# The odd chunks of the rwkv chunk stage kept on exchanged partition halves

## The chip, the cores and the metric

One core of a Trainium2 chip runs the kernel. The metric is the time of one execution on the device in microseconds (us); for several runs the median is given.

## What is computed

Twelve layers over 256 tokens of width 1024, in fp32. Each layer is a mixer and a feed-forward part; two of the mixers (rwkv, r = 0 and 1) are the recurrence that the change touches. Cut to its core, per head of 64:

```python
def step(state, inp):
    r_t, w_t, k_t, v_t, kk_t, a_t = inp
    sa = einsum('bhvk,bhk->bhv', state, kk_t)
    state = state * w_t - sa * (kk_t * a_t) + v_t * k_t      # outer products
    return state, einsum('bhvk,bhk->bhv', state, r_t)
_, y = lax.scan(step, zeros(B, 16, 64, 64), (rh, wh, kh, vh, kk, a))
y = ((y - mu) * rsqrt(var + eps)) * ln_w + ln_b             # per head
y = y + sum(rh * kh * r_k) * vh
out = (y * g) @ w_out
```

## The kernel before, in words

The layers run one after the other; weights stream in 512 KB units over the SP queue into rings, ScalarE and VectorE split each into a high and a low part, and TensorE runs three matmuls of 128x128 by 256 for each pair of blocks. In an rwkv layer the scan over 256 tokens is replaced by four chunks (CHN) of CH = 64 tokens. Sixteen heads of 64 are laid out in pairs: a tile [128, 8, 64] holds heads 2n on partitions 0 to 63 and 2n+1 on 64 to 127, so every product of the chunk stage is sixteen products of 64x64 (each_head, slices h), one for each n and half. In fp32 each is two weight loads and two matmuls in the trace. A product that reads its operands from half a and writes half b of PSUM uses the quarter (a, b) of the array. Most groups use h for both: they alternate between quarters (0,0) and (1,1).

The stage, in the order in which rwkv_pe (L301) issues it, by hand, on TensorE:
- to_tokens (L427), 12 groups: v, k and b of four chunks turned by the identity into banks B[0] to B[3]; ScalarE's tokens (L857, copies at L863) brings them to v_tok, kb_tok, bb_tok. Groups 4 to 7 wait for kb_done (VectorE, L1170), 8 to 11 for bb_done.
- score_part (L453, matmuls at L467): per chunk four half groups of 64x128; VectorE's mask (L1180, at L1182) multiplies them into scb and sck, and adds the unit matrix (L1188) and the turned level 0 (L1191) after part 1. Chunks 0 and 1 come first, the eight parts of chunks 2 and 3 two to a level of chunks 0 and 1.
- levels: the inverse of a unit triangular 64x64 matrix is built by doubling. level_product (L494) gives L·X for chunks a and a+1, the even chunk on (h, h), the odd one on (h, other(h)), so that successive matmuls go round all four quarters; VectorE's factor (L1193) multiplies by the level's mask into Qc; level_update (L509) makes the new X; ScalarE's copy_x (L866, at L869) brings it to Xc for even, then for odd; level_turned (L527) turns it and copy_turned (L871, at L874) copies it to XTc. level_product and level_turned wait for both copy_x.
- the chain over the chunks: right (L549), solve (L566), outputs_known (L577), outputs (L589), state (L599), with VectorE's carry (L1199) after each state, and the head norm of each chunk's result (head_mean, centre, centred_square, head_square, deviation, gained, normed). It lies between the levels of chunks 2 and 3, in an order written out by hand at L669 to L719. The queues of ScalarE (L911 to L982) and VectorE (L1239 to L1299) are written out by hand too, and each engine works strictly in its order. gn_std, st_ready, u_ready and the like are semaphores that count through both layers.

All of the stage is straight code without loops: some 1900 matmuls and as many weight loads in a layer, each an instruction of its own. After it, out_unit (L627) starts when the last norm is done.

```python
                for n, h in each_head():
                    even = mm(b0[h, n, :], scb[a][h, n, CH:2 * CH], Xc[a][h, n, :], start=True, stop=True)
                    odd = mm(b1[other(h), n, :], scb[a + 1][h, n, CH:2 * CH], Xc[a + 1][h, n, :], start=True, stop=True)
```

Of the kernel before, what the change touches and what calls it, by code (L numbers as in the profile page):

```python
# [145 lines left out]
def build_program(nc, layers, x_in, wa, wd, tab_in, vec_in, na_in, out):  # L146
# [6 lines left out]
    with ctx:  # L153
# [55 lines left out]
        for n in ("const_loaded tab_loaded x_loaded x_added sq_ready ssum_ready std_ready h_ready a_used d_used "  # L209
# [8 lines left out]
                  "v_final rk_ready rk_sum bonus_ready gain_ready tok_mm tok_ready score_mm score_ready lt_ready xt_ready "  # L218
# [59 lines left out]
        def score_bank(c, i):  # L278
            return level_bank(c, i % 3) if c < 2 else B[6 + i % 2]
# [21 lines left out]
        def rwkv_pe(pe, L, product):  # L301
# [114 lines left out]
            def each_head():  # L416
                for n in range(KT):
                    for e in range(2):
                        yield n, slice(HD * e, HD * e + HD)
# [3 lines left out]

            def ident_of(h):
                return T("ident")[h, h]

            def to_tokens(i):  # L427

                c, j = i % CHN, i // CHN
                if i >= 4:  # L430
                    pe.wait_ge(s["tok_ready"], 12 * r + i - 3)
                b = eight(B[i % 4][:, :])
                for n, h in each_head():
                    src = (qkv[h, 16 + n, tok(c)], qkv[h, 8 + n, tok(c)], oT[h, n, tok(c)])[j]
                    last = mm(b[h, n, :], src, ident_of(h), start=True, stop=True)  # L435
                last.then_inc(s["tok_mm"], 1)
# [4 lines left out]
            for i in range(4):  # L441
                to_tokens(i)
            pe.wait_ge(s["kb_done"], r + 1)
            for i in range(4, 8):
                to_tokens(i)
            pe.wait_ge(s["bb_done"], r + 1)
            for i in range(8, 12):
# [5 lines left out]
            def score_part(c, i):  # L453

                g = 4 * (c - 2) + i
                if g in (0, 1):
                    pe.wait_ge(s["bonus_ready"], 4 * r + 3 + g)
                elif g > 1:
                    pe.wait_ge(s["score_ready"], 16 * r + 7 + g)
                elif i == 3:  # L460
                    pe.wait_ge(s["score_ready"], 16 * r + 4 * c + 1)
                b = score_bank(c, i)[:, :].rearrange("p (n t) -> p n t", n=4)
                for n in range(4):
                    for h in (slice(0, HD), slice(HD, P)):
                        m = 4 * (i % 2) + n
                        left = qkv[h, 8 + m, tok(c)] if i >= 2 else oT[h, m, tok(c)]
                        last = mm(b[h, n, :], left, qkv[h, m:m + 25:24, tok(c)], start=True, stop=True)  # L467
                last.then_inc(s["score_mm"], 1)
# [2190 lines left out]
```

## Time and profile before

| | us |
|---|---|
| median of 3 runs (lowest, highest) | 2318.24 (2310.27, 2321.24) |
| the profiled execution | 2314.36 |
| its span, first to last instruction | 2312.3 |
| TensorE busy in it | 2195.0 (95%) |
| VectorE, ScalarE busy | 1548.9, 1209.7 |
| mean granted clock of TensorE | 0.989 |

The span runs from the first to the last instruction of the profiled execution; 2.1 us of that execution lie around it. Times on the rows are counted from the start of the span. Matmuls overlap in their pipeline, so a busy TensorE isn't one at its peak, and "issue" as the end of an idle time means that the engine waited for nothing that the profile shows. x is a count of instructions; mean times are in ns. The chunk stages lie at 134.5 to 262 us and at 1291 to 1415 us.

### The profile page before, as it was taken

To read this page: it belongs to the slowest core of one execution; us is meant where nothing else is said; L and a number is where in the kernel's file an instruction comes from. 1 tells how busy PE (TensorE), PEld (TensorE's weight loads), DVE (VectorE), ACT (ScalarE), POOL (GpSimd) and SP (SyncE) were. 2 spreads that over 40 slices of the span, in tenths; PEclk is the share of its full clock that TensorE was granted. 3 is DMA by queue.
4 is the path that set the end of the run, shared out by engine and by line. 5 is a ranking of instruction groups with operands and counts; after the bars stand their busy time and mean duration, and the time that the engine had idled before them with its cause. 6 is when DMAs were issued, how large, how long until landed. Compare 5 with 4: busy or idle time off the path is not lost. (4 is left out here: it accounts for less than half of the span.)

```text
span 2312.3 us, 55947 instructions
## 1 busy us (share of the span) xinstructions
PE 2195.0 (95%) x23136; PEld 2101.8 (91%) x23136; DVE 1548.9 (67%) x2397; ACT 1209.7 (52%) x2065; POOL 36.3 (2%) x51
## 2 busy tenths in 40 slices
PE   6898899999999999999989988999999999999998
PEld 6887799999999988899978878999998999888998
DVE  7753565566655688665588635655776777876776
ACT  5734454455544447644468335544676444776443
POOL 0000000000000011000000000000100000100000
PEclk9899999999999999999989999999999999999999
DMA  5310354534455433355433103555334554434553
GB/s 204 128 48 4 111 190 164 191 128 130 168 180 188 144 119 128 124 202 188 159 101 128 48 5 111 191 180 187 133 111 137 188 194 155 146 119 143 185 190 109
DMA packets 88436, 327.16 MB, mean 141 GB/s; under 512 B 9808, under 2 KB 9936, under 8 KB 87632
## 3 DMA queue, kind: packets, MB, share of 16 engines
q1 hardware_dynamic: 87984, 322.66, 41.3%
q8 instruction: 129, 2.11, 0.4%
q0 software_dynamic: 288, 2.10, 0.3%
q14 instruction: 35, 0.29, 0.0%
HBM read 323.67 MB, written 1.05 MB: 140 GB/s over the span
## 5 line engine op out<-in xcount | busy, mean ns | idle before, releaser
L2122 PE MATMUL bank<-h_split,w_split 128*128 128x256 f32 x3176 | 913.1, 287 | 12.9 <-DVE h_split L2341 7.2
L2123 PE MATMUL bank<-h_split,w_split 128*128 128x256 f32 x3176 | 898.3, 283 | 0.0
L2124 PE MATMUL bank<-h_split,w_split 128*128 128x256 f32 x3176 | 897.8, 283 | 0.0
L2310 DVE TENSOR_TENSOR w_split<-ring_a,w_split 128x1024 fp32r<-128x1024 f32 x474 | 568.2, 1225 | 194.6 <-ACT w_split L2207 193.0
L2122 PEld LDWEIGHTS bank<-h_split,w_split 128*128 128x128 f32 x3176 | 603.3, 190 | 24.8 <-DVE h_split L2341 11.3
L2123 PEld LDWEIGHTS bank<-h_split,w_split 128*128 128x128 f32 x3176 | 599.1, 189 | 1.4
L2124 PEld LDWEIGHTS bank<-h_split,w_split 128*128 128x128 f32 x3176 | 598.3, 188 | 0.0
L2207 ACT ACTIVATE w_split<-ring_a 128x1024 fp32r<-128x1024 f32 x474 | 483.3, 1050 | 44.1 <-PE bank L636 23.7
L2144 PE MATMUL bank<-act_split,d_split 128*128 128x256 f32 x1008 | 285.3, 283 | 3.8 <-DVE act_last L2402 2.4
L2145 PE MATMUL bank<-act_split,d_split 128*128 128x256 f32 x1008 | 285.1, 283 | 0.0
L2146 PE MATMUL bank<-act_split,d_split 128*128 128x256 f32 x1008 | 285.0, 283 | 0.0
L2274 ACT ACTIVATE work<-work 128x256 f32<-128x256 f32 x88 | 36.9, 419 | 347.8 <-DVE work L2380 347.8
L2144 PEld LDWEIGHTS bank<-act_split,d_split 128*128 128x128 f32 x1008 | 193.1, 192 | 4.6 <-DVE act_last L2402 2.8
L2146 PEld LDWEIGHTS bank<-act_split,d_split 128*128 128x128 f32 x1008 | 193.1, 192 | 0.0
L2145 PEld LDWEIGHTS bank<-act_split,d_split 128*128 128x128 f32 x1008 | 192.9, 191 | 0.0
L2380 DVE TENSOR_TENSOR work<-bank,work 128x512 f32<-128x512 f32 x132 | 91.0, 689 | 151.3 <-PE bank L2124 150.7
L2377 DVE TENSOR_TENSOR d_split<-ring_d,d_split 128x1024 fp32r<-128x1024 f32 x126 | 153.6, 1219 | 2.5 <-ACT d_split L2271 2.5
L2271 ACT ACTIVATE d_split<-ring_d 128x1024 fp32r<-128x1024 f32 x126 | 131.5, 1044 | 0.0
L2277 ACT ACTIVATE work<-work 128x256 f32<-128x256 f32 x44 | 18.4, 418 | 179.6 <-DVE work L2394 179.6
L2398 DVE TENSOR_TENSOR work<-work 128x256 f32<-128x256 f32 x132 | 56.2, 426 | 64.0 <-ACT work L2274 42.7
L2402 DVE TENSOR_TENSOR act_split<-work,act_split 128x256 fp32r<-128x256 f32 x126 | 53.6, 426 | 61.0 <-ACT act_split L2280 61.0
L2280 ACT ACTIVATE act_split<-work 128x256 fp32r<-128x256 f32 x126 | 52.6, 418 | 62.0 <-DVE work L2398 62.0
(292 smaller groups left out, 3243.7 us busy)
## 6 DMA issues: line engine op xcount, KB each, us to landing
ring_a<-wa SPq DMA_DIRECT2D x474, 512.0 KB, 4.0
ring_d<-wd SPq DMA_DIRECT2D x132, 512.0 KB, 4.3
tab_sb<-tab SPq DMA_DIRECT2D x1, 2384.0 KB, 13.3
hT<-na POOLq DMA_DIRECT2D x2, 1024.0 KB, 5.1
xT<-x SPq DMA_DIRECT2D x1, 1024.0 KB, 4.9
out<-xT SPq DMA_DIRECT2D x1, 1024.0 KB, 3.9
vec_sb<-vec SPq DMA_DIRECT2D x1, 288.0 KB, 4.9
tab_sb<-tab SPq DMA_DIRECT2D x1, 65.0 KB, 4.7
```

The costliest lines, as they stand in the source:

```text
L2122: mm(dst, w[:, 0, ks], x[:, 0, k, :], start=(k == 0), stop=False)
L2123: mm(dst, w[:, 0, ks], x[:, 1, k, :], start=False, stop=False)
L2124: last = mm(dst, w[:, 1, ks], x[:, 0, k, :], start=False, stop=(k == KT - 1))
L2144: mm(o, w[:, 0, ms], x[:, 0, :], start=(first and m % 2 == 0), stop=False, skip_group_check=True)
L2145: mm(o, w[:, 0, ms], x[:, 1, :], start=False, stop=False, skip_group_check=True)
L2146: return mm(o, w[:, 1, ms], x[:, 0, :], start=False, stop=final, skip_group_check=True)
L2207: A(w_split[:, u % 4, 0, :], ring_a[:, u % 4, :], ACT.Copy).then_inc(s["w_hi"], 1)
L2271: A(d_split[:, q, 0, :], ring_d[:, q, :], ACT.Copy).then_inc(s["dn_hi"], 1)
L2310: v.tensor_tensor(w_split[:, u % 4, 1, :], ring_a[:, u % 4, :], w_split[:, u % 4, 0, :].bitcast(f32), ALU.subtract).then_inc(s["w_lo"], 1)
L2377: v.tensor_tensor(dd[:, 1, :], ring_d[:, q, :], dd[:, 0, :].bitcast(f32), ALU.subtract).then_inc(s["dn_lo"], 1)
L2380: v.tensor_tensor(work[:, 2 * q:2 * q + 2, :], B[4 + q][:, :].rearrange("p (a b) -> p a b", a=2), inv_rms().unsqueeze(1).broadcast_to([P, ...
L2398: v.tensor_tensor(work[:, 2 * q + 1, :], work[:, 2 * q, :], work[:, 2 * q + 1, :], ALU.mult)\
```

## The change

The odd chunks' tokens (v_tok, kb_tok, bb_tok) and scores (scb, sck) are kept on exchanged halves: head 2n on partitions 64 to 127 and 2n+1 on 0 to 63. to_tokens and score_part now make two chunks at once, an even one on (h, h) and an odd one on (h, other(h)), matmul by matmul in turn. What then reads odd tokens or scores takes them from side(c, h), and in odd chunks a sum in PSUM has parts from different quarters: such parts are separated by a wait of TensorE for its own earlier part (parts_done). In right, outputs_known and state of odd chunks the order of parts changes with it. VectorE copies the odd chunk's second and third token blocks (5, 7, 9, 11) and the odd chunks' new X (copy_x), which ScalarE did before. The scores of chunks 2 and 3 are made in one group after each of four level updates.

```diff
@@ score_bank
-            return level_bank(c, i % 3) if c < 2 else B[6 + i % 2]
+            return level_bank(c, i % 3) if c < 2 else B[6 + c % 2]
@@ to_tokens
                 if i >= 4:
-                    pe.wait_ge(s["tok_ready"], 12 * r + i - 3)
-                b = eight(B[i % 4][:, :])
+                    pe.wait_ge(s["tok_ready"], 8 * r + (i - 2 if i < 8 else i // 2 + 1))
+                if i >= 8:
+                    pe.wait_ge(s["tok_side"], 4 * r + (i - 6) // 2)
+                b0, b1 = eight(B[i % 4][:, :]), eight(B[i % 4 + 1][:, :])
                 for n, h in each_head():
...
+                    even = mm(b0[h, n, :], block(i % CHN), ident_of(h), start=True, stop=True)
+                    odd = mm(b1[other(h), n, :], block(i % CHN + 1), ident_of(h), start=True, stop=True)
@@ score_part
+                    even = mm(b0[h, n, :], left(a), qkv[h, m:m + 25:24, tok(a)], start=True, stop=True)
+                    odd = mm(b1[other(h), n, :], left(a + 1), qkv[h, m:m + 25:24, tok(a + 1)], start=True, stop=True)
@@ level_zero
-                    pe.wait_ge(s["score_ready"], 16 * r + 4 * c + 4)
+                    pe.wait_ge(s["score_ready"], 16 * r + 7 + c)
@@ right
+                    for n, h in each_head():
+                        g = side(c, h)
+                        last = mm(b[h, n, :], sck[c][g, n, CH:2 * CH], v_tok[g, c, n, :],
+                                  start=(n == 0), stop=(c == 0), skip_group_check=True)
+                    if c % 2:
+                        last.then_inc(s["parts_done"], 1)
+                if c and second:
+                    if c % 2:
+                        parted(c if c == 1 else 4)
@@ outputs_known
                 if c:
                     for n, h in each_head():
+                        last = mm(y_of(c, h, n), state_[h, n, :], qkv[h, n, tok(c)],
+                                  start=(n == 0 or (c == 3 and n == 4)), stop=False, skip_group_check=True)
+                    if c % 2:
+                        last.then_inc(s["parts_done"], 1)
+                        parted(2 if c == 1 else 5)
@@ state
+                    if c == 1:
+                        last.then_inc(s["parts_done"], 1)
+                        parted(3)
@@ order on TensorE
-            for c in (0, 1):
-                for i in range(4):
-                    score_part(c, i)
+            for i in range(4):
+                score_part(0, i)
...
                 level_update(0, lv)
-                score_part(2 + (lv - 1) // 2, (lv - 1) % 2 * 2)
+                score_part(2, lv - 1)
                 level_product(0, lv + 1)
                 level_turned(0, lv)
-                score_part(2 + (lv - 1) // 2, (lv - 1) % 2 * 2 + 1)
...
             level_product(2, 2)
+            right(1, second=False)
             level_turned(2, 1)
-            right(1)
+            right(1, first=False)
...
             state(2)
+            right(3, second=False)
             outputs(2)
-            right(3)
+            right(3, first=False)
@@ order on ScalarE
-            for i in range(12):
+            for i in (0, 1, 2, 3, 4, 6, 8, 10):
                 tokens(i)
...
                 copy_x(0, lv)
-                copy_x(1, lv)
@@ VectorE
+            def copy_x(c, lv):
+                q = 2 * r + c // 2
+                dve.wait_ge(s["xn_mm1"], 4 * q + lv)
+                v.tensor_scalar(Xc[c], eight(level_bank(c, 1)[:, :]), 1.0, None, ALU.mult)\
+                    .then_inc(s["xn_ready1"], 1)
@@ order on VectorE
-            for c in (0, 1):
-                for i in range(4):
-                    mask(c, i)
+            for i in (5, 7, 9, 11):
+                tokens(i)
+            for i in range(4):
+                mask(0, i)
+                mask(1, i)
...
             for lv in range(1, 5):
-                mask(2 + (lv - 1) // 2, (lv - 1) % 2 * 2)
+                copy_x(1, lv)
+                mask(2, lv - 1)
                 factor(0, lv + 1)
                 factor(1, lv + 1)
-                mask(2 + (lv - 1) // 2, (lv - 1) % 2 * 2 + 1)
+                mask(3, lv - 1)
...
             carry(0)
+            copy_x(3, 1)
             factor(2, 2)
             factor(3, 2)
             centre(0)
             gained(0)
+            copy_x(3, 2)
             factor(2, 3)
             factor(3, 3)
             normed(0)
             carry(1)
+            copy_x(3, 3)
             factor(2, 4)
             factor(3, 4)
             centre(1)
+            copy_x(3, 4)
             factor(2, 5)
```

## Rows read from the trace of the kernel before

**Rows 1.** Windows: stretch, us, busy us (instructions) by engine, clock, DMA share, GB/s.
```profile
core 0: us, PE busy (x) PEld busy (x) DVE busy (x) ACT busy (x) POOL busy (x), PEclk, DMA share, GB/s
147.00:162.00 15.00, 14.51 (x293) 11.92 (x288) 11.64 (x18) 1.42 (x2) 0.00 (x0) 1.00 0.01 3
190.00:240.00 50.00, 41.82 (x1604) 36.93 (x1600) 14.65 (x23) 19.40 (x35) 0.00 (x0) 1.00 0.02 4
```
**Rows 2.** Timeline of the tokens: start, us, engine, line, count, idle before and releaser.
```profile
134.46 7.54 PEld L435 LDWEIGHTS bank<-tab_sb,qkv 64*64 64x64 f32 x256
135.50 1.23 DVE L1170 TENSOR_TENSOR qkv<-qkv,ring_d 128x1024 f32<-128x1024 f32 x1
...
145.92 0.60 ACT L863 ACTIVATE hT<-bank 128x512 f32<-128x512 f32 x1 [0.34 <-PE bank L435]
...
146.57 1.96 PE L467 MATMUL bank<-qkv,oT 64*64 64x128 f32 x32 [0.70 <-ACT hT L863]
```
**Rows 3.** Windows within one level_product, for its line L504, then for L505.
```profile
164.50:165.50 1.00, 0.93 (x31) 0.96 (x32) 1.00 0.00 0
...
164.50:165.50 1.00, 0.92 (x31) 0.93 (x32) 1.00 0.00 0
```
**Rows 4.** DMA view of 190 to 240 us, then of 178 to 181 in 40 slices.
```profile
q8 instruction: 13, 0.21, 1.7%
...
GB/s 0 218 0 0 0 0 0 0 0 0 0 0 0 0 0 0 0 0 0 0 0 0 0 0 0 0 0 0 0 0 0 0 0 0 0 0 0 0 0 0
```
**Rows 5.** Timeline of TensorE: restarts after an idle time that ends in "issue".
```profile
180.64 0.21 PE L534 MATMUL bank<-tab_sb,planes 64*64 64x64 f32 x1 [1.76 <-issue]
...
186.22 0.27 PE L504 MATMUL bank<-planes 64*64 64x64 f32 x1 [0.67 <-issue]
...
189.57 0.65 PE L467 MATMUL bank<-qkv 64*64 64x128 f32 x8 [0.95 <-issue]
...
223.67 0.27 PE L505 MATMUL bank<-planes 64*64 64x64 f32 x1 [0.52 <-issue]
...
227.56 0.63 PE L593 MATMUL bank<-planes,work 64*64 64x64 f32 x15 [1.70 <-issue]
...
236.76 0.21 PE L534 MATMUL bank<-tab_sb,planes 64*64 64x64 f32 x1 [1.77 <-issue]
...
1378.31 0.85 PE L613 MATMUL bank<-work,hT 64*64 64x64 f32 x22 [0.34 <-issue]
...
1381.81 0.21 PE L535 MATMUL bank<-tab_sb,planes 64*64 64x64 f32 x1 [1.07 <-issue]
```
**Rows 6.** Timeline of VectorE: first and last masks of chunks 0 and 1.
```profile
147.71 0.69 DVE L1182 TENSOR_TENSOR planes<-bank,tab_sb 128x512 f32<-128x512 f32 x1 [9.85 <-PE bank L467]
...
150.65 2.48 DVE L1182 TENSOR_TENSOR planes<-bank,tab_sb 128x512 f32<-128x512 f32 x4
153.16 0.69 DVE L1188 TENSOR_TENSOR planes<-planes,tab_sb 128x512 f32<-128x512 f32 x1
153.77 1.28 DVE L1182 TENSOR_TENSOR planes<-bank,tab_sb 128x512 f32<-128x512 f32 x2
```
**Rows 7.** Timeline: a level's update, copies, product; next update; product of the last level.
```profile
162.13 0.27 PE L522 MATMUL bank<-planes 64*64 64x64 f32 x1
...
163.34 1.09 ACT L869 ACTIVATE planes<-bank 128x512 f32<-128x512 f32 x2 [2.34 <-PE bank L522]
...
164.57 0.24 PE L504 MATMUL bank<-planes 64*64 64x64 f32 x1 [0.41 <-ACT planes L869]
...
167.93 0.24 PE L522 MATMUL bank<-planes 64*64 64x64 f32 x1 [0.40 <-ACT planes L874]
...
233.26 0.24 PE L504 MATMUL bank<-planes 64*64 64x64 f32 x1 [0.21 <-ACT planes L869]
```
**Rows 8.** Source view of L1064, VectorE's tensor_scalar out of PSUM: min/median/max ns.
```profile
L1064 DVE TENSOR_SCALAR work<-bank x2: 692/692/692, 53.3 to 1206.7; 128x512 f32<-128x512 f32 x2
```
**Rows 9.** Timeline of VectorE: carry(1) and centre(1), first layer, then second.
```profile
223.05 0.69 DVE L1201 TENSOR_TENSOR work<-bank,small 128x512 f32<-128x512 f32 x1 [5.14 <-PE bank L613]
...
233.09 0.69 DVE L1218 TENSOR_TENSOR oT<-oT,bank 128x512 f32<-128x512 f32 x1 [7.05 <-PE bank L620]
...
1379.28 0.69 DVE L1201 TENSOR_TENSOR work<-bank,small 128x512 f32<-128x512 f32 x1 [5.34 <-PE bank L613]
...
1387.63 0.69 DVE L1218 TENSOR_TENSOR oT<-oT,bank 128x512 f32<-128x512 f32 x1 [6.12 <-PE bank L620]
```

More of the change, by code:

```diff
@@ L414, in rwkv_pe, with each_head @@
                 one(22 + m, 16 + m, 5)
-            def each_head():
-                for n in range(KT):
+            def each_head(count=KT):
+                for n in range(count):
                     for e in range(2):
@@ L451, in counts, with score_part, left @@
                 return 2 * r + c // 2, c % 2
[L453 to L459, printed above, removed]
-                elif i == 3:
[L461 to L468, printed above, removed]
+            def score_part(a, i):
+                if a:
+                    if i == 0:
+                        pe.wait_ge(s["bonus_ready"], 4 * r + 4)
+                    else:
+                        pe.wait_ge(s["score_ready"], 16 * r + 8 + 2 * i)
+                elif i == 3:
+                    pe.wait_ge(s["score_ready"], 16 * r + 2)
+                b0, b1 = [score_bank(a + t, i)[:, :].rearrange("p (n t) -> p n t", n=4) for t in range(2)]
+                for n, h in each_head(4):
+                    m = 4 * (i % 2) + n
+                    def left(c):
+                        return qkv[h, 8 + m, tok(c)] if i >= 2 else oT[h, m, tok(c)]
+                    even = mm(b0[h, n, :], left(a), qkv[h, m:m + 25:24, tok(a)], start=True, stop=True)
+                    odd = mm(b1[other(h), n, :], left(a + 1), qkv[h, m:m + 25:24, tok(a + 1)], start=True, stop=True)
+                even.then_inc(s["score_mm"], 1)
+                odd.then_inc(s["score_mm"], 1)
             def level_zero(c):
@@ L490, in turned_zero @@
                 for n, h in each_head():
-                    last = mm(b[other(h), n, :], Xc[c][h, n, :], ident_of(h), start=True, stop=True)
+                    last = mm(b[h, n, :], Xc[c][other(h), n, :], ident_of(other(h)), start=True, stop=True)
                 last.then_inc(s["xt_mm1"], 1)
@@ L572, in solve @@
                 for n, h in each_head():
-                    g = other(h) if c % 2 else h
-                    last = mm(b[h, n, :], XTc[c][g, n, :], rhs_[g, n, :], start=True, stop=True)
+                    last = mm(b[side(c, h), n, :], XTc[c][h, n, :], rhs_[h, n, :], start=True, stop=True)
                 last.then_inc(s["u_mm"], 1)
@@ L592, in outputs @@
                 for n, h in each_head():
-                    last = mm(y_of(c, h, n), u_[h, n, :], scb[c][h, n, 0:CH], start=False, stop=True,
+                    g = side(c, h)
+                    last = mm(y_of(c, h, n), u_[g, n, :], scb[c][g, n, 0:CH], start=False, stop=True,
                               skip_group_check=True)
@@ L612, in state @@
                 for n, h in each_head():
-                    last = mm(b[h, n, :], bb_tok[h, c, n, :], u_[h, n, :], start=False, stop=True,
+                    g = side(c, h)
+                    last = mm(b[h, n, :], bb_tok[g, c, n, :], u_[g, n, :], start=False, stop=True,
                               skip_group_check=True)
```

81 lines of the change are left out of this document (43 added, 38 removed).

## Prediction

> **What bounds the kernel now.** The windows view comes first: the change touches only the chunk stage of the two rwkv layers (134.5 to 262 us and 1291 to 1415 us), about 252 of 2312 us. There TensorE is busy most of the time at a granted clock of 1.00 (2.4 GHz), DMA carries 3 to 4 GB/s, and ScalarE and VectorE are far from full except for VectorE while the first scores are masked (11.64 of 15 us) [rows 1]. So the question is what TensorE waits for.
>
> The timeline tells how fast it goes. Turning twelve token blocks begins with 256 matmuls and their weight loads in 7.54 us: 29.4 ns each, and the copies on ScalarE (0.60 us) wait for it [rows 2]. These groups alternate between two 64x64 quarters of the array, (0,0) and (1,1). The level products alternate over all four, and 62 of their matmuls fit in 0.93 us: 15 ns each [rows 3]. That doubling is what tokens and scores could get.
>
> But the DMA view and the idle rows show a second limit. In 50 us with 1604 matmuls (and as many weight loads) the instruction queue moved 13 packets of 16 KB: one per 128 matmuls or so [rows 1, 4]. TensorE's idle rows that end in "issue" lie the same 128 matmuls apart and fall just behind such packets: the packet at 178.1 us (second of 40 slices of 3 us) is followed by the restart at 180.64 [rows 4, 5]. Where nothing else holds TensorE up, restarts are 3.35 us apart (186.22 to 189.57), elsewhere 3.5 to 3.9 (1378.31 to 1381.81, 227.56 back to 223.67) [rows 5]. I read this as a supply of instructions of one packet per 3.35 to 3.9 us, the next one asked for only when the sequencer is some 40 matmuls into the present one. A packet lasts 3.75 us at 29.4 ns and 1.9 us at 15 ns. So **the fast form can run ahead only as far as instructions are already there; over a long stretch it is held to about 27 ns**, little better than the slow form.
>
> **The change part by part**, first rwkv layer / second layer. The number of matmuls is unchanged.
>
> *Tokens.* Six pairs of 64 matmuls at 15 ns need 0.95 us each in place of 1.87. Without a supply limit: pairs 0 and 1 are through at 136.4; pair 2 waits for kb_done, 136.73 [rows 2]; four more pairs end at 140.7, the last pair of copies (0.60 on ScalarE, 0.69 on VectorE beside it, by the PSUM to SBUF tensor_scalar [rows 8]) at 141.6 to 142.0; the scores start 4.6 us before the 146.57 of now [rows 2]. With the limit: counting matmuls back from the restart at 180.64, packets end 172 and 300 matmuls into the tokens. The first is reached at 137.45 and supplied at 138.3, the second at 140.25 and supplied at 141.8, so the scores start at 144.0: **-2.55 / -3.0** (in the second layer packets end 138 and 266 matmuls in; the second costs 1.4 us, the third, in the scores, 0.6). Bounds: -4.6 each, and 0 if the supply took it all.
>
> *Scores of chunks 0 and 1.* TensorE needs half of its 7 us, but VectorE has eight masks and three additions or products, 0.64 to 0.69 us each, and they fill 147.71 to 155.05 nearly without a gap [rows 6]: it is the bound already. Nothing is gained; mask(0,3) now comes last but one, so level_zero(0) waits for it: +0.15. Sum so far -2.4 / -2.9.
>
> *Levels of chunks 0 and 1.* Now: update at 162.13, two copies on ScalarE end at 164.43, product at 164.57, 2.44 us [rows 7]. With one copy on each engine the product can start at +2.0 (0.69 on VectorE, [rows 8]): 0.4 per level, the chain 5.35 in place of 5.8 us. But a level has 224 matmuls, 1.75 packets, so 5.9 to 6.2 us of supply. Walking the four levels packet by packet, with 3.5 us for each and later where a wait stands before the request: last_turned comes **0.8 / 0.4 us** earlier beyond the shift above. The halved scores of chunks 2 and 3 were under the ScalarE copies and stay there. Bounds: -3 (3.35 per packet throughout) to +1.5 per layer (two more waits ahead of a request).
>
> *Levels of chunks 2 and 3.* TensorE waits on ScalarE's copies hardly at all here, so the parallel copy brings nothing. Its place in VectorE's queue costs. copy_x(3,3) stands behind carry(1), which waits for state(1): 223.05 to 223.74, so the copy ends at 224.4 and level_product(2,4), which now goes on behind a packet at 223.67, starts 0.7 to 1.3 us later; in the second layer carry runs 1379.28 to 1379.97, the product starts at 1380.7 in place of 1379.1 and the packet behind it is asked for later by as much and a little more: +2.1 [rows 5, 9]. copy_x(3,4) stands behind centre(1), 233.09 to 233.78: product at 234.5 where it was 233.26, +1.2; second layer centre at 1387.63, +0.65, since a packet stall of 0.35 gives some back [rows 7, 9]. **+2.5 / +2.75**. Bounds 0 (all taken up in stalls of "issue") and +3.4.
>
> *Waits of TensorE on itself* (parts_done): five a layer, needed as accumulating parts now come from other quarters. Those in right(1) and right(3) have a group of 32 or 64 other matmuls ahead of them. In outputs_known(1), state(1) and outputs_known(3) the array must empty: last matmul 0.22, then 0.14 as from a copy's end to the product (164.43 to 164.57) [rows 7]: 0.36 each. What is queued behind is the second half of the same group; who waits is the solve and its copies. The first two lie ahead of packet stalls that take them up; the third counts: **+0.35 / +0.35**. No row shows such a wait; bounds 0 and 1.5 each, if the sequencer, stopped, asks for the next packet later.
>
> *Moved.* right(1)'s first half goes ahead of level_turned(2,1), right(3)'s ahead of outputs(2). copy_y(2) comes 0.9 later and head_mean(2) 0.1: nothing. ScalarE loses 12 copies a layer and isn't the bound. SP and POOL queues are not passed; weight DMAs are untouched.
>
> **Sum**: -2.4 - 0.8 + 2.5 + 0.35 = -0.35, and -2.9 - 0.4 + 2.75 + 0.35 = -0.2: -0.6 us. The profiled execution took 2314.4 us (span 2312.3 and 2.1 around it), 3.9 below the median of the runs, which spread over 11 us. So 2313.8 for it and 2317.6 for a median; I say 2317.5.
>
> **Rivals.**
> *The supply binds less than I read* (2305, chance 0.16). For it: I infer the request rule from gaps only. Then a layer gains 4.45 in tokens, 4 x 0.9 in the first levels (0.4 of chain, and as much again of the "issue" time of now, 0.67 to 1.76 us a stall [rows 5]), and loses half of 2.6 to the queue and 0.35 to emptying: -6.4 a layer, -12.8. Against: restarts 128 matmuls apart, in both layers.
> *Stopped sequencer* (2326, 0.10), the slower side: each of three emptying waits a layer delays the next packet by what the sequencer had run ahead, 1.3 us and more, not 0.36. Then 3 x 1.3 + 3.4 (both queue waits in full) = 7.3 a layer against 3.2 and 3.3 won early: +8.1. With both queue waits in full the gain is gone at once, and half a per cent is lost from 1.9 us a wait on. For it: where a product had to wait early in a packet (233.26), the next stall was 1.77 us, among the longest [rows 5, 7]. Against: later slack is there to absorb it.
> *The pairs run no faster* (2323, 0.03): the token and score pairs share the quarters otherwise than the products do, and stay at 29 ns. Then only the costs remain (2.85 and 3.1 a layer, less 0.4 in the levels), +5.5. Against: order of quarters is exactly that of level_product.
> *A floor per matmul* (2318, 0.03): matmuls of the token groups start no closer than halfway between the two rates, 22 ns. Six pairs then take 8.5 us, with 0.4 for kb_done and 1 for the last copies the scores start at 144.4: -2.2 a layer, 0.7 more on the sum. Rows 3 show 15 ns and speak against it.
> The Trainium skill, "TensorE: Matmul & The Clock Gate", section "Wait — 56ns, not 53.3ns?", says that start-to-start never drops below about 25 ns however small the matmul. By that an estimate for the tokens is 9.6 us and a gain of some 1.5 us a layer, the total 2 us above the forecast. This case's trace does not agree where quarters alternate (15 ns).
>
> **How the numbers follow.** Forecast 0.68, with its own range 2311 to 2322. Half a per cent, 11.6 us, is about what a measurement here can tell from no change. The faster rival passes it in 0.11, the slower one in 0.06: same 0.83. For 8 in 10 the range reaches down to 2306, into the first rival's cases (tokens at their bound of -4.45 and levels at -3 with the costs as forecast: -9 to -10, 2308), and up to 2325, most of the slower one's.
>
> **What would show it.** In the profile after: L435's group at 15 ns in bursts with new idle of type "issue" between; scores starting 2.5 to 3 us earlier; first masks back to back as now; levels 5.9 to 7 us apart; VectorE's copy right behind carry(1) and centre(1) and a product on TensorE waiting for it; as many instruction packets as now. The prediction is wrong if the tokens gain over 4 us a layer, if "issue" time vanishes, or if idle time behind the parts_done waits exceeds 0.5 us each.

## The result, and the profile after

The changed kernel is slower, by a little more than the measurement can miss: a median of 2323.41 us (2317.17 to 2329.25, 20 runs) against 2317.16 us for the kernel before in 20 runs beside it. The ratio is 1.0027, 95% interval 1.0020 to 1.0035: +6.2 us, where -0.6 us was forecast. It lies inside the stated range (2306 to 2325) and within the half per cent named there, yet on the other side of zero. The profiled execution took 2325.95 us with a span of 2323.9 us and a mean granted clock of 0.981 (before: 2312.3 us and 0.989). The ratios here and below leave out two executions of the kernel before (5486 and 3492 us), which ran in a slow state.

**The tokens went as worked out.** The first fence is the timeline of TensorE in the changed kernel (start, us, engine, line, form, count, idle before and what ended it). L443 and L444 are the even and the odd half of a pair in to_tokens, L478 is the first line of a score group.

```profile
134.84 0.22 PE L443 MATMUL bank<-tab_sb,qkv 64*64 64x64 f32 x1
...
134.90 0.22 PE L443 MATMUL bank<-tab_sb,qkv 64*64 64x64 f32 x1
...
138.46 0.27 PE L444 MATMUL bank<-tab_sb,qkv 64*64 64x64 f32 x1 [0.46 <-issue]
...
141.86 0.21 PE L444 MATMUL bank<-tab_sb,oT 64*64 64x64 f32 x1 [1.04 <-issue]
...
144.24 0.29 PE L478 MATMUL bank<-qkv,oT 64*64 64x128 f32 x1 [0.87 <-ACT hT L894]
...
1307.07 0.29 PE L478 MATMUL bank<-qkv,oT 64*64 64x128 f32 x1 [0.83 <-ACT hT L894]
```

Four matmuls (two L443, two L444) start from 134.84 on, before the next one at 134.90: 15 ns each, against 29.4 [rows 2]. Then come two stalls that end in "issue", restarting at 138.46 and 141.86 where 138.3 and 141.8 had been forecast. The scores start 9.56 us after the first token (134.68) in place of 12.11 [rows 2], in the second layer 8.76 us: -2.55 and -3.35.

**Then the lead is lost.** The view of TensorE's waits groups its idle time by who ended it: us in total, times, longest. First the changed kernel, its first chunk stage.

```profile
PE bank L548 <- issue: 5.2, 3, 2.2
PE bank L536 <- ACT planes L905: 3.8, 3, 1.3
PE bank L493 <- DVE planes L1215: 3.7, 1, 3.7
PE bank L517 <- DVE planes L1229: 3.0, 2, 1.5
PE bank L664 <- DVE rw_o_split L1341: 2.7, 1, 2.7
```

The same view of the kernel before has these in the same places:

```profile
PE bank L534 <- issue: 3.5, 2, 1.8
...
PE bank L504 <- ACT planes L869: 2.4, 6, 0.7
...
PE bank L522 <- ACT planes L874: 1.2, 3, 0.4
...
PE bank L480 <- DVE planes L1182: 0.5, 1, 0.5
```

Three waits have grown. level_zero (L493, formerly L480) waits 3.7 us for the masks where it waited 0.5: TensorE is through with the scores early and the masks on VectorE are not, which was forecast. The updates (L536, formerly L522) wait 1.3 us each for copy_turned where it was 0.4, since the second score group that lay there now lies ahead of the product. The products wait 1.5 us twice for VectorE's copy (L1229), which was forecast too. In the two stages together TensorE's waits on others rise from 12.6 to 29.3 us, and its busy time falls by some 12 us.

**And the clock falls**, which the prediction never spoke of. The windows view (stretch, us, busy us and instructions of five engines, granted clock, DMA share, GB/s) of the changed kernel:

```profile
151.00:155.00 4.00, 3.01 (x61) 3.04 (x63) 2.13 (x4) 0.00 (x0) 0.00 (x0) 0.57 0.02 4
168.00:172.00 4.00, 4.00 (x140) 4.00 (x143) 2.00 (x3) 0.60 (x1) 0.00 (x0) 0.57 0.02 4
182.00:186.00 4.00, 3.15 (x91) 2.94 (x95) 0.69 (x1) 2.85 (x6) 0.00 (x0) 0.57 0.01 4
240.00:244.00 4.00, 4.00 (x60) 2.67 (x60) 0.00 (x0) 2.76 (x5) 0.00 (x0) 0.57 0.01 4
1315.00:1319.00 4.00, 3.74 (x65) 3.70 (x66) 1.49 (x4) 0.00 (x0) 0.00 (x0) 0.57 0.01 4
1332.00:1336.00 4.00, 4.00 (x134) 3.88 (x133) 1.45 (x3) 1.06 (x3) 0.00 (x0) 0.57 0.02 4
1346.00:1350.00 4.00, 4.00 (x142) 4.00 (x144) 1.48 (x4) 1.13 (x3) 0.00 (x0) 0.58 0.03 6
```

A clock of 0.57 over 4 us means 3.4 us at half (1.2 GHz) and the rest at full (2.4 GHz). The kernel before has 1.00 in all seven windows and in rows 1. The first fall (at 151.3 us) comes just ahead of the end of this wait in the timeline, the fifth (at 1315.2) at the end of its like in the second layer:

```profile
151.99 0.37 PE L493 MATMUL bank<-tab_sb,planes 64*64 64x64 f32 x2 [3.72 <-DVE planes L1215]
...
1315.26 1.02 PE L493 MATMUL bank<-tab_sb,planes 64*64 64x64 f32 x14 [4.02 <-DVE planes L1215]
```

**The two copies in VectorE's queue** answer to rows 9 and to the product in rows 7. VectorE, then TensorE:

```profile
223.34 0.69 DVE L1240 TENSOR_TENSOR work<-bank,small 128x512 f32<-128x512 f32 x1 [5.24 <-PE bank L643]
223.94 0.68 DVE L1229 TENSOR_SCALAR planes<-bank 128x512 f32<-128x512 f32 x1
...
233.85 0.69 DVE L1257 TENSOR_TENSOR oT<-oT,bank 128x512 f32<-128x512 f32 x1 [6.53 <-PE bank L650]
234.46 0.68 DVE L1229 TENSOR_SCALAR planes<-bank 128x512 f32<-128x512 f32 x1
```

```profile
224.77 0.24 PE L517 MATMUL bank<-planes 64*64 64x64 f32 x1 [1.49 <-DVE planes L1229]
...
235.29 0.24 PE L517 MATMUL bank<-planes 64*64 64x64 f32 x1 [1.47 <-DVE planes L1229]
```

carry ends, the copy follows, and the product starts 0.15 us after the copy. Both products lose 1.5 us.

The stages by section, worked out from the starts of the groups in the timelines (us, first / second layer). S is first token to first score, Z on to level_zero, U on to update(0,1), L on to last_turned(0), R on to the first matmul of out_unit. "Half" is the time at half clock in the stage, "sum" both stages. The labels are explained with the experiments; "changed" is the changed kernel run again beside others.

| kernel | S | Z | U | L | R | half | sum |
|---|---|---|---|---|---|---|---|
| before | 12.11 / 12.11 | 7.04 / 7.04 | 8.52 / 8.52 | 27.93 / 27.30 | 72.16 / 69.24 | 0 / 0 | 252.0 |
| after | 9.56 / 8.76 | 7.75 / 8.20 | 9.08 / 9.39 | 29.72 / 28.08 | 74.62 / 72.80 | 15.1 / 11.3 | 258.0 |
| changed | 9.58 / 8.91 | 7.76 / 8.20 | 10.22 / 9.26 | 28.67 / 28.04 | 74.95 / 72.52 | 10.2 / 7.7 | 258.1 |
| copy_only | 12.11 / 12.11 | 7.04 / 7.04 | 8.51 / 8.52 | 27.70 / 27.61 | 72.78 / 72.51 | 0 / 1.7 | 255.9 |
| waits_before | 12.11 / 12.11 | 7.04 / 7.04 | 8.51 / 8.52 | 28.51 / 27.02 | 70.25 / 70.21 | 1.4 / 0 | 251.3 |
| scalar_x | 9.88 / 8.85 | 8.03 / 8.21 | 9.46 / 9.33 | 27.11 / 27.32 | 72.92 / 71.20 | 3.4 / 6.8 | 252.3 |
| queue | 10.39 / 8.57 | 9.01 / 8.74 | 9.45 / 10.37 | 29.20 / 26.58 | 71.28 / 70.33 | 10.2 / 6.8 | 253.9 |
| warm | 10.13 / 11.09 | 9.09 / 7.76 | 7.86 / 7.87 | 26.09 / 27.32 | 73.62 / 70.33 | 4.0 / 1.7 | 251.2 |
| small_fill | 9.58 / 9.96 | 7.75 / 9.10 | 7.87 / 9.45 | 26.62 / 26.69 | 75.60 / 70.33 | 3.4 / 6.8 | 252.9 |
| phase_early | 10.50 / 11.95 | 8.05 / 7.83 | 9.47 / 9.40 | 25.73 / 28.14 | 74.21 / 72.97 | 6.8 / 7.6 | 258.2 |
| fill_zero | 9.48 / 10.52 | 7.76 / 7.75 | 7.87 / 10.21 | 25.87 / 28.05 | 74.74 / 71.09 | 0.9 / 12.0 | 253.3 |
| fill_levels | 9.48 / 10.24 | 7.76 / 9.05 | 10.08 / 9.46 | 26.35 / 25.86 | 74.75 / 71.08 | 7.3 / 6.8 | 254.1 |
| before_bonus | 12.11 / 12.11 | 9.05 / 9.05 | 6.90 / 6.90 | 28.16 / 27.59 | 69.93 / 69.75 | 0.6 / 0 | 251.6 |
| queue_warm | 9.62 / 10.53 | 9.10 / 7.76 | 7.87 / 7.86 | 25.24 / 27.06 | 72.25 / 70.25 | 5.2 / 0.8 | 247.5 |
| queue_bonus | 10.03 / 8.57 | 7.76 / 8.48 | 6.90 / 6.90 | 25.29 / 28.21 | 71.70 / 71.79 | 6.8 / 8.2 | 245.6 |
| twice | 21.31 / 19.47 | 7.75 / 8.58 | 9.48 / 10.54 | 28.17 / 26.52 | 75.82 / 74.01 | 6.8 / 6.8 | 281.7 |
| queue_bonus_split | 9.85 / 9.03 | 7.76 / 8.21 | 6.90 / 6.90 | 26.34 / 27.05 | 70.85 / 70.46 | 3.4 / 3.4 | 243.4 |

The sum of the changed kernel is 6.0 us above before, close to the difference of the medians (6.2), so the two stages can hold all of it. Each line of the table is one execution, and outside the stages executions differ too: the spans of before and after are 11.6 us apart, 5.6 of it outside. 4.0 of that lies between the stages (1028.9 and 1032.9 us, with 30.7 and 42.9 us at half clock), and waits_before, which has the order of before, shows the same 1033.0 and 42.9. The medians below rest on 7 to 12 runs, but for twice, which is one run.

### The profile page after: what moved, and what is told of

It is laid out like the page before. It is cut to its first block, busy times and chain, and to the rows that moved or that the text cites. A ratio compares the mean times of both kernels' runs of the same rounds, so it can differ in the third digit from the quotient of the medians.

```text
span 2323.9 us, 55963 instructions
## 1 busy us (share of the span) xinstructions
PE 2189.5 (94%) x23136; PEld 2093.2 (90%) x23136; DVE 1564.4 (67%) x2421; ACT 1196.3 (51%) x2041; POOL 35.9 (2%) x51
## 4 chain that ended last, share of the span: by engine, by line
PE 81%; DVE 10%; ACT 5%; issue 3%; DMA 0%; SPq 0%; ACTq 0%; DVEq 0%
PE bank L2168 15%; PE bank L2169 15%; PE bank L2170 15%; PE bank L2190 5%; PE bank L2191 5%; PE bank L2192 5%; DVE w_split L2356 2%; ACT w_split L2253 1%; PE bank L1581 1%; PE bank L1583 1%; PE bank L1582 1%; PE bank L1520 1%; PE bank L1548 1%; PE bank L1485 1%; DVE work L1039 1%
## 5 line engine op out<-in xcount | busy, mean ns | idle before, releaser
L2168 PEld LDWEIGHTS bank<-h_split,w_split 128*128 128x128 f32 x3176 | 602.9, 190 | 26.7 <-DVE h_split L2387 11.3
```

Source lines behind the costliest of these rows:

```text
L2168: mm(dst, w[:, 0, ks], x[:, 0, k, :], start=(k == 0), stop=False)
```

## The experiments

Ratios are to the kernel before on the same chip, with their 95% interval. The changed kernel itself gave 2323.97 us again, 1.0026 (1.0017 to 1.0035).

> The changed kernel itself, as the measure for the three beside it. Both theories: 6 us above the kernel before (2323), with six or seven stretches of 3.4 us at half clock in the two chunk stages.

**The copies' place in VectorE's queue.** Only the order of two steps in the changed kernel:

```diff
-            carry(1)
             copy_x(3, 3)
+            carry(1)
...
-            centre(1)
             copy_x(3, 4)
+            centre(1)
```

> The changed kernel, with VectorE's copy_x(3,3) put ahead of carry(1) and copy_x(3,4) ahead of centre(1) in its queue; nothing else. Queue theory: in the changed kernel level_product(2,4) and level_product(2,5) each start after an idle of TensorE of 1.47 to 1.49 us that ends with VectorE's copy, in both layers (223.29 to 224.77, 233.81 to 235.29; 1385.65 to 1387.14, 1396.4 to 1397.91). These four idles go, and with the later requests for instruction packets 2 to 3 us a layer: 4 to 6 us below the changed kernel, about level with the kernel before. Clock theory: the loss sits in the stretches at a granted clock of 0.5, seven of 3.4 us in the two stages; this edit touches at most the one near 240 us, and gives 1 us or less beside the idles, which stalls for instructions take up.

Measured: 2317.20 us, 1.0000 (0.9987 to 1.0012), 6 us below the changed kernel. R falls by 3.3 and 2.5 us against after, where the prediction had put 2.5 and 2.75 for these two places. The term is right in place and, over both layers, about right in size.

**All copies back on ScalarE**, the rest of the change kept:

```diff
@@ ScalarE, copy_x
-                act.wait_ge(s["xn_mm0"], 4 * q + lv)
+                act.wait_ge(s[f"xn_mm{t}"], 4 * q + lv)
@@ ScalarE's order
                 copy_x(0, lv)
+                copy_x(1, lv)
@@ VectorE's order
-                copy_x(1, lv)
```

> The changed kernel with all copies of the new inverse back on ScalarE, even then odd (tokens, scores, halves and parts_done waits as changed). Queue theory: the idles before level_product(2,4) and (2,5) go, -2 to -3 us a layer; the levels of chunks 0 and 1 get the second ScalarE copy back, +0.4 each if nothing else holds them, +0.8 to 1.6 a layer: in all 1 to 4 us below the changed kernel. Clock theory: the longer copies add idle time before each product and the clock falls as often as in the changed kernel or more: no gain on it, or 1 us slower.

Measured: 2318.07 us, 1.0002 (0.9993 to 1.0011): the same as before, and as the reordered queue. So exchanged halves without VectorE's copies gain nothing that shows either.

**The copies on VectorE alone**, put into the kernel before (nothing exchanged): the edit above turned round, with VectorE's copy_x and its places as in the change.

> The kernel before with only the copy of the odd new inverse moved to VectorE, at the places in its queue that the change gives it. Queue theory: the two idles of about 1.5 us a layer appear, +2 to +3 us a layer, against 0 to 1.6 gained in the levels of chunks 0 and 1: 1 to 5 us above the kernel before. Clock theory: scores still stand before each level update and no idle of 3.7 us arises, so the clock stays at 1.0 in the levels: then the change's other half holds the greater part of the 6 us, and this kernel is within 2 us of the kernel before.

Measured: 2321.35 us, 1.0015 (1.0006 to 1.0024). This part alone costs about 4 us; by sections R grows by 0.6 us in the first layer and 3.3 in the second. Its products wait as in the changed kernel (timeline of TensorE in this kernel):

```profile
224.26 0.24 PE L504 MATMUL bank<-planes 64*64 64x64 f32 x1 [1.47 <-DVE planes L1191]
...
234.29 0.24 PE L504 MATMUL bank<-planes 64*64 64x64 f32 x1 [1.47 <-DVE planes L1191]
```

Its section L is 27.70 / 27.61 against 27.93 / 27.30 before, almost wholly at full clock: the parallel copies bring -0.2 and +0.3 us. The -0.8 and -0.4 forecast for them aren't there even where nothing else has changed.

**TensorE's waits for itself alone**, three a layer in the kernel before:

```diff
@@ outputs_known
+                if c % 2:
+                    last.then_inc(s["parts_done"], 1)
+                    pe.wait_ge(s["parts_done"], 3 * r + c)
@@ state
+                    if c == 1:
+                        last.then_inc(s["parts_done"], 1)
+                        pe.wait_ge(s["parts_done"], 3 * r + 2)
```

> The kernel before with three waits of TensorE for its own earlier group in each rwkv layer, in outputs_known(1), state(1) and outputs_known(3), where the change has them; nothing else. The forecast's price: 0.36 us of idle each, the first two taken up by stalls for instructions: +0.7 us in all. The rival of the stopped sequencer: each wait delays the next instruction packet by 1.3 us or more: +4 to +8 us, and stalls that end in issue grow behind each wait.

Measured: 2317.91 us, 1.0002 (0.9992 to 1.0011): the rival of the stopped sequencer (1.3 us and more a wait, 7.8 for six) falls. The forecast of 0.35 a layer lies within the interval and can't be told from nothing.

**How fast instructions come.** Every token product of the changed kernel is made twice (192 products more a layer, 384 matmuls; the second overwrites the first: extra work, the same values):

```diff
-                for n, h in each_head():
+                for n, h in [nh for _ in range(2) for nh in each_head()]:
```

> The changed kernel with every matmul of to_tokens issued twice (same result), 384 more matmuls and as many weight loads a layer in groups that go round all four quarters. Packet theory: three more packets of instructions a layer, so the tokens take 3 x 3.35 to 3 x 3.9 us more, 10 to 11.7 us a layer, 27 to 30 ns per added matmul, with new idle that ends in issue. If the rate of the array alone counted: 15 ns, 5.8 us more a layer.

Measured, one run: 2347.83 us. The first score starts 21.31 and 19.47 us after the first token, 11.75 and 10.71 later than in after. That is 31 and 28 ns for each added matmul, though in a burst they still start 15 ns apart. Timeline of TensorE in this kernel, a stall and the first score:

```profile
138.78 0.21 PE L444 MATMUL bank<-tab_sb,qkv 64*64 64x64 f32 x1 [0.99 <-issue]
...
156.33 0.29 PE L478 MATMUL bank<-qkv,oT 64*64 64x128 f32 x1 [0.88 <-ACT hT L894]
```

So the rival "supply binds less" falls, and so does "a floor per matmul" at 22 ns: the burst is at 15, the average at the supply.

**Filling TensorE's waits with long matmuls.** Fillers are extra work whose results nobody reads: a product of 128x128 by 512, three after the scores of chunks 0 and 1 and one before each of updates 2 to 4.

```diff
+            def filler(b):
+                a = TAB["stick_neg"][0]
+                mm(b[:, :], T("ident"), tab[:, a:a + 512], start=True, stop=True)
...
                 score_part(0, i)
+            for i in range(3):
+                filler(B[6 + i % 2])
             level_zero(0)
...
             for lv in range(1, 5):
+                if lv > 1:
+                    filler(B[1])
                 level_update(0, lv)
```

> The changed kernel with filler matmuls (identity by a constant table, 128x512, result never read, 1 us each by the 128x512 matmuls of the bonus sums): three between the scores of chunks 0 and 1 and level_zero(0), where TensorE idles 3.72 and 4.02 us, and one ahead of level_update in levels 2 to 4, where it idles 1.2 to 1.3 us. Clock theory: the stretches of 3.4 us at half clock near level_zero and in these levels (151, 168, 182 and 1315, 1332, 1346 us in the changed kernel) mostly go; a level_zero group takes 1.1 us again in place of 1.98, and the stage is 1.5 to 2.5 us a layer shorter: 3 to 5 us below the changed kernel. Queue theory alone: the levels of chunks 0 and 1 are bound by copies and by instruction packets at either clock; fillers fit in idle time and the time is that of the changed kernel, or 1 us more.

Measured: 2317.41 us, 0.9998 (0.9987 to 1.0008). Extra work made the kernel 6 us faster. In its profile level_zero's wait has shrunk to this row, the clock doesn't fall there, and the half-clock time of both stages is 5.7 us instead of 26.4 and 17.9:

```profile
154.36 0.86 PE L493 MATMUL bank<-tab_sb,planes 64*64 64x64 f32 x22 [0.94 <-DVE planes L1223]
```

**The same fillers, tiny** (64x64 by 64, the same twelve matmuls a stage in the trace), which take hardly any time:

```diff
-                mm(b[:, :], T("ident"), tab[:, a:a + 512], start=True, stop=True)
+                mm(b[0:HD, 0:HD], T("ident")[0:HD, 0:HD], tab[0:HD, a:a + HD], start=True, stop=True)
```

> The changed kernel with fillers at the same places and in the same number as in the run with long fillers (three ahead of level_zero, one ahead of the updates of levels 2 to 4), but 64x64 by 64, 15 to 30 ns a matmul in place of about half a us. Clock theory: they fill nothing, the idle of 3.7 us stays and with it the stretches at half clock: as the changed kernel, 2322 to 2324. Rival, that the long fillers helped by shifting where the instruction packets end: the same instructions shift them as much, so 2317 as with the long fillers.

Measured: 2318.53 us, 1.0007 (0.9997 to 1.0018): nearly as much. The clock theory alone had said 2322 to 2324 and missed. Twelve extra matmuls also move every later packet's end by twelve matmuls against the program, so two causes were open.

**Telling them apart.** Tiny fillers (extra work again) in three other places of the changed kernel: six ahead of the first score group; six after the last; two before each of updates 2 to 4.

```diff
@@ phase_early
+            for i in range(6):
+                filler(B[6 + i % 2])
             for i in range(4):
                 score_part(0, i)
@@ fill_zero
             for i in range(4):
                 score_part(0, i)
+            for i in range(6):
+                filler(B[6 + i % 2])
@@ fill_levels
+                if lv > 1:
+                    filler(B[1])
+                    filler(B[1])
                 level_update(0, lv)
```

> The changed kernel with six small fillers in a row (64x64 by 64, twelve matmuls in the trace, extra work, results unused) ahead of the first score group of each layer; no gap of TensorE is filled. It moves every later packet boundary by twelve matmuls against the program. Packet place theory (the small fillers helped because they moved the packet boundaries away from the level chains): 2317 to 2319.5, ratio to before 1.0000 to 1.0010. Gap theory (they helped because they lay in or next to TensorE's waits and kept the granted clock up): scores 0.3 us later for the fillers, nothing gained: 2322.5 to 2325, ratio 1.0025 to 1.0035, half clock in the profile as long as in the changed kernel (18 to 26 us for both stages).

> The changed kernel with the six small fillers (extra work) all between the last score group and level_zero, none before the updates. Packet place theory: as with the early fillers, 2317 to 2319.5, ratio 1.0000 to 1.0010, since all later boundaries move by the same twelve. Gap theory with the gap before level_zero deciding: the same time, but then the early fillers give nothing. If the waits before the updates decide: 2322.5 to 2324.5.

> The changed kernel with two small fillers (extra work) before each of updates 2, 3 and 4 and none ahead of level_zero. Packet place theory: only the boundaries from the second level on move, by four, eight and twelve; most of the stage has the same places as with twelve, 2318 to 2321, ratio 1.0005 to 1.0015. Gap theory with the waits before the updates deciding: 2318 to 2319. If the gap before level_zero decides: 2322.5 to 2324.5.

Measured: 2320.14 us, 1.0021 (1.0011 to 1.0031); 2318.79 us, 1.0015 (1.0004 to 1.0025); 2316.12 us, 1.0007 (0.9997 to 1.0018). None settles it, and the intervals overlap: phase_early lies between the two theories, and fill_levels by its ratio (about 2319 us) fits both. The sections say more. phase_early and fill_zero have the same packet ends in the levels, and their L agrees to 0.15 us in both layers (25.73 / 28.14, 25.87 / 28.05) although one has 6.8 / 7.6 us at half clock and the other 0.9 / 12.0. Against the changed kernel (28.67 / 28.04) the same shift took 2.9 us off the first layer's levels and nothing off the second's. But U differs by 1.6 us in the first layer (9.47 against 7.87), with the same instructions and packet ends in it and only the clock different. The windows of the same 8 us from just before level_zero, phase_early and then fill_zero:

```profile
153.00:157.00 4.00, 3.79 (x66) 3.19 (x67) 2.04 (x4) 0.00 (x0) 0.00 (x0) 0.69 0.02 4
157.00:161.00 4.00, 4.00 (x101) 2.66 (x100) 2.44 (x4) 0.03 (x1) 0.00 (x0) 0.89 0.01 4
```

```profile
151.00:155.00 4.00, 3.13 (x67) 2.62 (x68) 2.70 (x5) 0.00 (x0) 0.00 (x0) 1.00 0.01 4
155.00:159.00 4.00, 4.00 (x102) 2.67 (x101) 2.69 (x5) 0.60 (x1) 0.00 (x0) 1.00 0.02 4
```

Over all kernels with the changed order, U is 9.08 to 10.54 in all fourteen layers (seven profiles) where nothing lies in level_zero's wait; with tiny fillers there it is 7.87 in two layers of four and 9.45 and 10.21 in the others; with long ones 7.86 or 7.87 in four of four. The clock orders them all: the six layers without half-clock time in U have 7.86 or 7.87, the other sixteen have 2.7 to 5.8 us of it and are longer by 0.45 to 0.47 us for each us. Z follows the clock too: it is 9.01 to 9.10 instead of 7.75 in the five layers where 3.3 or 3.4 us at half clock lie in the scores (queue, warm and queue_warm in the first layer, small_fill and fill_levels in the second).

**Useful work in the wait.** The bonus sums of chunks 0 and 1 (L676, four matmuls of 128x128 by 512) need nothing of level_zero; with the queue order from above:

```diff
+            bonus_sum(0)
+            bonus_sum(1)
             level_zero(0)
             level_zero(1)
-            bonus_sum(0)
-            bonus_sum(1)
```

> The kernel with the two copies moved in VectorE's queue, and bonus_sum(0) and (1), four long matmuls of 2 us together, put ahead of level_zero(0) into TensorE's idle time there, no instruction added. Clock theory: idle before level_zero falls from 3.7 to about 1.7 us and the fall near 151 and 1315 us goes; and 2 us of work leave the way between level_zero(1) and the first product: 2 to 3 us a layer, so 4 to 6 us below the kernel before (about 2312). If only VectorE sets this stretch (masks, factor, bonus in its queue): the product waits for factor(1,0) and bonus work just moves: 0 to 2 us below the kernel before.

Measured: 2311.86 us, 0.9982 (0.9972 to 0.9992). U is 6.90 in both layers, all at full clock, and level_zero's wait is 2.1 us. The same move in the kernel before:

> The kernel before with bonus_sum(0) and (1) ahead of level_zero(0), nothing else. There TensorE has no idle before level_zero(0), it goes on from the scores without a gap. If the gain of 5 us of the version with bonus sums moved comes from filling an idle time that only the change opened: 0 here, or 1 to 2 us slower a layer as level_zero waits for them. If it comes from their place alone: 2 us a layer faster, 2313.

Measured: 2317.19 us, 0.9999 (0.9989 to 1.0009). There TensorE had no gap at that place: what U gains (1.6 us), Z pays (2.0 us).

Then the score groups of chunks 2 and 3 in halves, one before the product and one before the next update, and their masks behind the factors:

```diff
-                score_part(2, lv - 1)
+                score_part(2, lv - 1, 0)
                 level_product(0, lv + 1)
                 level_turned(0, lv)
+                score_part(2, lv - 1, 1)
```

> As the one before, and each group of scores of chunks 2 and 3 in two halves, one before the product and one before the next update as the kernel before had them, VectorE's two masks behind the level's two factors. Clock theory: idle ahead of each update falls from 1.2 to 0.3 us, no falls within the levels: 1 to 2 us a layer more than the one before gains, so 6 to 9 us below the kernel before (about 2309). Packet theory: levels take 1.75 packets, 5.9 to 6.2 us, either way, and nothing more is gained than by the one before.

Measured: 2311.83 us, 0.9973 (0.9961 to 0.9984), below both kernels (by 4.8 us against before by the medians, 6.3 by the ratio). Against queue_bonus alone the difference is within the intervals, so the split isn't shown to help; its profile has less half-clock time (6.8 against 15.0 us).

Last, the queue order with the long fillers (extra work):

> The changed kernel with both the two copies ahead in VectorE's queue and the long fillers. Each alone took 6 us off. If queue and clock are separate losses, both together take 9 to 12 us off: 2311 to 2314, and the changed kernel's other parts (tokens on four quarters) show as a gain of 3 to 6 us on the kernel before. If they are one loss seen twice, or take from the same slack for instruction packets, no more than 7 us: 2316.

Measured: 2313.53 us, 0.9977 (0.9967 to 0.9987), 10.4 us below the changed kernel: the two remedies nearly add up (by the ratios 6.0 and 6.5 us alone, 11.4 together), so they mostly mend different things.

## Why the prediction was off

Two terms of the sum failed. The levels of chunks 0 and 1 were to gain 1.2 us over both layers and lost 2.6. And the way from level_zero to the first update was taken at full clock, with nothing in the sum for it, and lost 2.7 us to half clock.

**What bounds the kernel: right.** The instruction queue was the limit that the doubled rate ran into. In the changed kernel's window 190 to 240 us it moved 12 packets for 1544 matmuls, where rows 4 show 13 for 1604:

```profile
q8 instruction: 12, 0.20, 1.5%
```

The restarts came within 0.2 us of the walk through the packets, and doubling the tokens cost the supply's 28 to 31 ns a matmul.

**Tokens: right** (-2.55 forecast and measured in the first layer, -3.0 and -3.35 in the second).
The Trainium skill, "TensorE: Matmul & The Clock Gate", section "Wait — 56ns, not 53.3ns?", has a lower limit of about 25 ns from start to start. The trace doesn't agree where matmuls go round all four quarters (15 ns), and yet an average of 28 to 31 ns came out, for another reason.

**Scores: right at full clock.** Forecast +0.15 a layer. Z grew by 0.71 and 1.16, since level_zero(0) now waits for ten of eleven operations of VectorE instead of the first chunk's; it had started inside that chain before. But for the same reason the way behind it is shorter: at full clock U is 7.87 instead of 8.52. Z and U together would be 0.06 us longer in the first layer and 0.51 in the second. There the matmuls of the first score group stop for 0.3 us (1307.23 to 1307.53), and the first mask comes 0.45 us later behind its scores; the prediction had named such a stall in the scores, of 0.6. With the tokens, the first update would have come 2.5 / 2.8 us earlier, where the forecast's sum to this point was 2.4 / 2.9.

**level_zero: not in the sum at all.** The prediction let it follow the masks at full speed. The 3.7 and 4.0 us of idle ahead of it stood in its own arithmetic (TensorE needs half of VectorE's 7 us), but it asked only whether they bound, not what TensorE's clock does after them. U would have fallen from 8.52 to 7.87, as in warm; it rose to 9.08 and 9.39. So 1.2 and 1.5 us, 2.7 in all, are the price of the half clock.

**Levels of chunks 0 and 1: the step that failed most.** Forecast -0.8 / -0.4, L changed by +1.8 / +0.8, a miss of 3.8 us in all. About 1.3 of it is the parallel copy, which brought -0.2 / +0.3 in the kernel before too: a level that no packet end disturbs did get shorter (5.46 us, 5.80 before), but the four levels together did not. The walk "packet by packet" gave a gain smaller than what the position of the packets' ends alone makes. Twelve matmuls more moved L by 2.9 us in one layer and 0 in the other, and over all kernels with the change's order it lies between 25.2 and 29.7 us. The bound given (+1.5 a layer) was exceeded in the first layer. The loss in the first layer doesn't need the clock: changed and queue have no half-clock time in the first layer's L, and it is 28.67 and 29.20 us, with 6.1 and 6.4 us of idle in it that ends in "issue" and 4.6 and 4.5 of waits for other engines, against 3.5 and 3.1 before. How much the clock falls at 168, 182, 1332 and 1346 us add stays open. The changed kernel run again had one fall in these sections in place of four, and its two L came to 56.7 us instead of 57.8; in the second layer L was 28.05 with one fall and 28.08 with two, but 26.58 in queue without any. The position of the packets differs between these as well.

**The statement that the halved scores "stay there" under ScalarE's copies: wrong in detail.** They covered copy_turned before the next update; that wait went from 0.4 to 1.3 us. An undisturbed level is still shorter than before, and moving half of the scores back was not shown to help, so this isn't shown to be a net loss.

**Queue waits: right over both layers.** Forecast +2.5 / +2.75, R grew by 2.46 / 3.56 with the waits for itself in it (forecast together 2.85 / 3.1). Taking them out brought 6 us and 5.8 in the sections R. Copies alone cost 4 us in the kernel before, but hardly any of it in the first layer. That each layer fits so well is partly luck: with all copies on ScalarE and the order of before, R is 69.9 to 72.2 in the first layer and 69.2 to 70.2 in the second (before, waits_before, before_bonus), so stalls for instructions alone move it by up to 2 us.

**Waits for itself: right, or less.** Forecast 0.7 us for both layers; six such waits cost 0.5 us by the ratio, with an interval from -1.9 to +2.5.

The sum by sections against the forecast: S -0.35, Z +1.6, U +1.4 (the two together 3.0, of which 2.7 are the half clock), L +3.8 and R +0.1, which makes 6.5 us, nearly the whole miss (6.8 by the medians). The rivals did not hold it: the rival at 2326 comes near the measured time for a reason that the runs refute, and no rival was a clock that falls because TensorE finishes early.

## What to carry to other kernels

When an edit makes the engine that sets the pace faster just ahead of a wait for another engine, look at what lies in the new gap: here 3.7 to 4.1 us of idle were followed by half clock that cost 1.2 to 2.7 us each time, and useful work moved into the gap (the bonus sums), together with the copies' new place in the queue, turned a loss of 6 us into a gain of 4. A copy moved to another engine must be placed in that engine's queue by what it stands behind: behind a wait for a later product it cost more than running the copies in parallel brought. And where small instructions are bound by their own supply, a few instructions more or less anywhere shift the stalls by microseconds, so the effect of one edit should be measured with the count changed as well before a mechanism is believed.

## What the runs showed of the hardware

- TensorE's instructions come in 16 KB packets, one for about 128 matmuls with their weight loads (12 packets and 1544 matmuls in 50 us). 384 added matmuls cost 11.75 and 10.71 us, 28 to 31 ns each, while matmuls in a burst started 15 ns apart.
- The granted clock fell to half (1.2 GHz) for 3.4 or 6.8 us at a time in a stage where it had been full throughout. Around level_zero this came in, or within 1.5 us behind, the idle time of 3.7 to 4.1 us in all fourteen layers with nothing in the gap (seven profiles), and in none of four with three long matmuls in it (0.9 to 1.1 us of idle left). Tiny matmuls in the gap left 3.1 to 3.5 us of idle and a fall in two layers of four. With 1.8 to 2.1 us of idle in front of level_zero the clock stayed full up to the first update (queue_bonus and queue_bonus_split, four layers).
- One us at half clock behind level_zero made the stretch 0.45 to 0.47 us longer (sixteen layers against six at full clock).
- Elsewhere falls have their own time in each execution: 26.4 us at half clock in one profile of the changed kernel and 17.9 in another, with stages of 258.0 and 258.1 us. They also came behind shorter idles, as the one at 182.0 us behind 2.2 us and the one at 1332.3 us behind 1.5 and 1.3.
- TensorE's wait for its own earlier part showed no cost that can be measured (six a kernel, +0.5 us by the ratio, interval -1.9 to +2.5).
